# Three RMS norms of a long Trainium2 kernel: x is turned unscaled and split from PSUM, the scale is applied behind the matrices, and the gated unit's blocks change their order

## The chip, the cores and the metric

The kernel runs on one core of one Trainium2 chip. The metric is the device time of one execution in microseconds, smaller being better. The engines are named as in the profile: PE (TensorE) multiplies matrices, PEld is its load of the stationary operand, DVE is VectorE, ACT is ScalarE, POOL is GpSimd, SP is SyncE.

## What is computed

Three residual layers over 256 tokens of width 1024, in fp32: layer 0 mixes by attention, layer 1 by a state-space unit (S5) whose output goes through a gated unit, and each ends in a feed-forward of width 4096. A third layer with conditioning, convolution, window attention and an expert part of 16,384 rows follows. What the change touches, cut from the reference:

```
def rms_norm(x, g):
    y = xf * lax.rsqrt(jnp.mean(xf * xf, axis=-1, keepdims=True) + EPS)
    return (y * g).astype(x.dtype)

def s5_mixer(...):
    ...
    val, gate = jnp.split(g @ w_glu, 2, axis=-1)
    return val * jax.nn.sigmoid(gate)

def sq_relu_mlp(h, w1, w2):
    return jnp.square(jax.nn.relu(h @ w1)) @ w2

for layer in range(DEPTH):                      # DEPTH = 2
    h = rms_norm(x, mix_norm_g[layer])
    ...                                         # attn_mixer begins with h @ w_in; or s5_mixer
    x = x + sq_relu_mlp(rms_norm(x, ffn_norm_g[layer]), w_ff1[layer], w_ff2[layer])
```

The norm has a scale per token, r = 1/sqrt(mean square + EPS), and a gain per channel, g. A product with h is r times the product with x * g; squared and relu'd it is r squared times.

## The kernel before

Every engine has a program written out by hand (`tensor_program`, `vector_program`, `scalar_program`, `gpsimd_program`, `sync_program`); the order of the work is the order of that code, and semaphores (`Signal`, `Bank`) join the programs. x lies in `xr`, 128 tokens by 2 by 1024.

**Matrices at fp32 precision.** Both operands of a large product are cut into a high part in fp32r (`w_hi`, `HH`) and a low rest (`w_lo`, `HL`); `three` (L523) issues hi*hi, hi*lo and lo*hi. Weights stream through a ring of four units of 512 KB (SP, L515), two chunks of 512 columns each. `cut_ahead` on ACT makes the high part (L1823), `cut_ahead` on DVE the low one (L1069), up to three chunks ahead of the chunk that PE is at, into four places; ACT may overwrite a place when PE has used it (`w_used`). `lin_tok` keeps the turned activations stationary and has eight chunks per block of 512 columns; `lin_T` keeps the weights stationary, two chunks per half (m) of a pair j of output blocks. In `ff1` a chunk is twelve matmuls of 256 columns. `weave` and `side` put small steps of other work between the chunks: in `ffn(0)` the tables of S5 (`s5_tables`, on PE, ACT and DVE), in `ffn(1)` the conditioning vector (`ada_step`: ACT fetches `w_ada`, DVE sums it).

**A norm** (`norm` in three programs; numbers 0 before `w_in`, 1 before `ff1_0`, 2 before S5, 3 before `ff1_1`, 4 and 5 later) is a chain over three engines: ACT squares both token halves with a sum; DVE takes mean and EPS; ACT the root; DVE the reciprocal and four scalings of x into `hn`; PE turns `hn` in sixteen 128x128 transposes (L544) into banks 4 to 7; DVE multiplies each bank by the gain into SBUF; ACT cuts HH, DVE cuts HL; only then `lin_tok` or `lin_T` begins:

```
for n in range(4):                                           # DVE, L1103
    ts(hn[:, t, half], xr[:, t, half], ss[:, t:t + 1], None, ALU.mult).then_inc(*scaled("hn", s, n))
tt(dst, pb(4 + n, 4, 128), B(g.unsqueeze(2), [128, 4, 128]), ALU.mult)
copy(HH[sl], hT[sl]).then_inc(*ahi_cut("norm", s, n))        # ACT
low(HL[place(3)], hT[place(3)], HH[place(3)], "norm", s, 3)  # DVE
```

**Around the norms.** At the start ACT issues both halves of x and then `small` (the identity for the transposes and the gains); SP waits for both halves of x before the first weights; `norm(0)` on PE waits for `small`. Before norm 1 stands `mix_out("w_o", ...)`: two blocks of eight chunks, each followed by two additions to x on DVE. Before norm 3 stands `glu`: blocks in the order values 0, gates 0, values 1, gates 1; behind each gates block ACT takes two sigmoids and DVE, per token half, multiplies by the values in PSUM and adds to x. `ffn` ends with four additions from PSUM to x (`add_to_x`).

## Time and profile before

| | |
|---|---|
| median of 3 runs | 1603.62 us (1602.17 to 1605.49) |
| profiled execution, its own time | 1605.25 us |
| its span in the profile | 1602.7 us |
| PE, PEld, DVE, ACT, POOL busy | 1475.8, 1361.2, 1166.7, 798.5, 326.9 us |
| DMA | 346.61 MB, 216 GB/s in the mean |

The span runs from the first to the last instruction of the profiled execution. PE is busy for 92% of it, so what is left lies in short stretches in which PE waits; a view by stretches shows them, and the timeline shows what fills them.

### The profile page before, as it was taken

How to read it: one execution, taken by the hardware profiler on the slowest of the kernel's cores; microseconds unless marked ns; L12 is line 12 of the kernel's file. 1: busy time of each engine (PE TensorE's matmuls, PEld its weight loads, DVE VectorE, ACT ScalarE, POOL GpSimd, SP SyncE). 2: the span in 40 equal slices, each digit the busy share in tenths (PEclk: the TensorE clock that was granted, in tenths of full speed). 3: DMA queues.
4: the chain of work that ended last, by engine and by line, in shares of the span. 5: the costliest groups of instructions: out<-in, count | busy, mean ns of one | idle time of the engine just before them, and what ended most of it. 6: DMA issues, size and time to landing. Idle time of an engine off the chain costs nothing.

```text
span 1602.7 us, 28608 instructions
## 1 busy us (share of the span) xinstructions
PE 1475.8 (92%) x10976; PEld 1361.2 (85%) x10976; DVE 1166.7 (73%) x2281; ACT 798.5 (50%) x1623; POOL 326.9 (20%) x380
## 2 busy tenths in 40 slices
PE   6788999998788999979879999999999989999998
PEld 5566998676777997858769899999999989999997
DVE  5575986575747887976775599367777768888887
ACT  4585786553655444545645210243333346666664
POOL 6520001000000000000000000178878811111110
PEclk9999999999999999989899999999999999999999
DMA  6214454453046888844235466699999968988884
GB/s 216 82 40 140 132 171 136 129 156 122 30 156 203 294 290 282 308 172 165 79 106 162 144 205 200 236 330 364 368 356 326 349 224 300 308 305 299 311 309 146
DMA packets 102197, 346.61 MB, mean 216 GB/s; under 512 B 11360, under 2 KB 11488, under 8 KB 101808
## 3 DMA queue, kind: packets, MB, share of 16 engines
q1 hardware_dynamic: 67680, 245.00, 45.8%
q0 software_dynamic: 19264, 70.84, 12.4%
q10 hardware_dynamic: 15120, 28.95, 5.5%
q8 instruction: 89, 1.46, 0.4%
q14 instruction: 44, 0.36, 0.1%
HBM read 343.70 MB, written 1.05 MB: 215 GB/s over the span
## 4 chain that ended last, share of the span: by engine, by line
PE 69%; DVE 14%; DMA 6%; ACT 5%; POOL 4%; issue 3%; ACTq 0%; DVEq 0%
PE ps L521 67%; DVE arena L1069 6%; ACT arena L1820 2%; DVE w_lo L1069 2%; DMA arena<-in_v_rows,arena 2%; POOL arena L2598 2%; POOL arena L2587 2%; DVE arena L1075 2%; DMA arena<-in_u_rows,arena 2%; ACT w_hi L1823 1%; DVE arena L1072 1%; DMA arena<-in_peer_v 1%; DVE act_hi_lo L1069 1%; ACT arena L1823 1%; PE ps L759 0%
## 5 line engine op out<-in xcount | busy, mean ns | idle before, releaser
L1069 DVE TENSOR_TENSOR w_lo<-arena,w_hi 128x512 fp32r<-128x512 f32 x680 | 457.0, 687 | 236.1 <-ACT w_hi L1823 232.8
L1823 ACT ACTIVATE w_hi<-arena 128x512 fp32r<-128x512 f32 x680 | 418.6, 626 | 360.7 <-PE ps L521 264.3
L521 PE MATMUL ps<-act_hi_lo,w_hi 128*128 128x256 f32 (+1 forms) x2496 | 567.8, 318 | 13.8 <-DVE act_hi_lo L1069 12.5
L521 PE MATMUL ps<-arena 128*128 128x192 f32 (+12 forms) x4952 | 520.7, 286 | 36.8 <-DVE arena L1069 11.3
L521 PEld LDWEIGHTS ps<-arena 128*128 128x128 f32 (+3 forms) x4952 | 484.3, 166 | 68.4 <-issue 26.1
L521 PE MATMUL ps<-act_hi_lo,w_lo 128*128 128x192 f32 (+1 forms) x1760 | 466.6, 265 | 0.0
L521 PEld LDWEIGHTS ps<-act_hi_lo,w_hi 128*128 128x128 f32 x2496 | 424.4, 191 | 19.2 <-issue 15.8
L521 PE MATMUL ps<-w_hi,act_hi_lo 128*128 128x512 f32 (+2 forms) x960 | 318.1, 403 | 33.3 <-ACT w_hi L1823 10.3
L521 PEld LDWEIGHTS ps<-act_hi_lo,w_lo 128*128 128x128 f32 x1760 | 339.0, 193 | 0.0
L521 PEld LDWEIGHTS ps<-w_hi,act_hi_lo 128*128 128x128 f32 x960 | 186.1, 195 | 83.1 <-issue 25.2
L1069 DVE TENSOR_TENSOR arena<-arena 128x512 f32<-128x512 f32 (+13 forms) x315 | 197.1, 631 | 43.6 <-ACT arena L1820 28.3
L521 PE MATMUL ps<-w_lo,act_hi_lo 128*128 128x512 f32 (+2 forms) x480 | 190.6, 397 | 0.0
L1823 ACT ACTIVATE arena<-ps 128x512 f32<-128x512 f32 (+16 forms) x202 | 81.6, 430 | 181.8 <-DVE arena L1069 132.1
L1820 ACT ACTIVATE arena<-arena 128x128 f32<-128x128 f32 (+7 forms) x300 | 140.8, 480 | 60.6 <-DVE arena L1069 23.6
L1075 DVE SCALAR_TENSOR_TENSOR arena<-arena 128x512 f32<-128x512 f32 (+6 forms) x176 | 152.4, 866 | 15.2 <-DMA arena<-in_v_rows,arena 11.0
L1820 ACT ACTIVATE arena<-ps 32x128 f32<-32x128 f32 (+20 forms) x201 | 80.3, 421 | 149.3 <-PE ps L521 147.4
L2587 POOL DMA_INDIRECT arena<-in_u_rows,arena x64 | 83.1, 1299 | 249.4 <-DVE arena L1696 223.6
L2587 POOL DMA_INDIRECT arena<-in_v_rows,arena x64 | 81.7, 1276 | 239.1 <-DVE arena L1075 183.7
L2439 POOL TENSOR_TENSOR arena<-arena 128x32 f32<-128x32 f32 (+1 forms) x122 | 44.6, 379 | 373.9 <-ACT arena L1823 343.4
L1713 DVE SCALAR_TENSOR_TENSOR arena<-arena 128x1024 f32<-128x1024 f32 x64 | 78.3, 1233 | 42.4 <-DMA arena<-in_u_rows,arena 27.3
L521 PEld LDWEIGHTS ps<-w_lo,act_hi_lo 128*128 128x128 f32 x480 | 93.6, 195 | 17.4 <-issue 0.5
L1069 DVE TENSOR_TENSOR arena<-ps,arena 128x512 f32<-128x512 f32 (+18 forms) x154 | 82.4, 552 | 24.6 <-PE ps L521 17.6
(81 smaller groups left out, 632.8 us busy)
## 6 DMA issues: line engine op xcount, KB each, us to landing
arena<-in_w_ff SPq DMA_DIRECT2D x128, 512.0 KB, 4.0
arena<-in_peer_u SPq DMA_DIRECT2D x128, 512.0 KB, 5.2
arena<-in_peer_v SPq DMA_DIRECT2D x128, 512.0 KB, 5.6
arena<-in_w_ada ACTq DMA_DIRECT2D x96, 256.0 KB, 4.4
arena<-in_w_glu SPq DMA_DIRECT2D x16, 512.0 KB, 3.6
arena<-in_peer_wq SPq DMA_DIRECT2D x16, 512.0 KB, 3.6
arena<-in_w_in SPq DMA_DIRECT2D x12, 512.0 KB, 3.6
arena<-in_w_conv SPq DMA_DIRECT2D x12, 512.0 KB, 3.6
```

The lines of the kernel that those rows point to most:

```text
L521: return e.matmul(o, l, r, start=start, stop=stop)
L1069: return e.tensor_tensor(o, a, b, op)
L1072: return e.tensor_scalar(o, a, s1, s2, op0, op1) if op1 is not None else e.tensor_scalar(o, a, s1, None, op0)
L1075: return e.scalar_tensor_tensor(out=o, in0=a, scalar=s, in1=b, op0=op0, op1=op1)
L1713: ins = e.scalar_tensor_tensor(out=slot, in0=slot, scalar=1.0, in1=row_h[:, g], op0=ALU.mult, op1=ALU.mult, accum_out=a)
L1820: return e.activation(o, a, f, **k)
L1823: return e.activation(o, a, ACT.Copy)
L2439: return e.tensor_tensor(o, a, b, op)
L2587: e.indirect_dma_start(row_slot(n), None, T[f"{kind}_rows"], bass.IndirectOffsetOnAxis(ap=row_at[:, p:p + 1].bitcast(U32), axis=0)).then_i ...
L2598: ins = e.tensor_scalar(ob[:, k, :], iota, ibT[:, n:n + 1], gT[:, n:n + 1], ALU.is_equal, ALU.mult)
```

## The change

What it does, part by part:

- **Norms 0, 1 and 3.** PE turns x itself (`turn_x`), sixteen transposes of 128 channels by 128 tokens; ACT cuts HH straight from PSUM with the gain as its per-partition scale (`cut_x`, eight instructions of 256 columns); DVE makes HL in one instruction, PSUM times gain less HH (`low_x`, eight). `hn`, the four scalings and the four multiplications by the gain are gone from these norms.
- **Their scale** moves behind the products. Norm 0: squares, root and reciprocal stand inside the first `w_in` block, and each of the four `proj` evictions multiplies by r. Norms 1 and 3: squares on ACT behind pair j = 2 of `ff1`, mean and reciprocal on DVE behind j = 6 (r squared, so no root), and the four additions at the end of the feed-forward become `stt` with that scale.
- **First half of x early.** `turn_half` puts eight transposes of norm 1 inside the second `w_o` block, `glu` eight of norm 3 inside its last block. The other eight follow the block.
- **First pair of ff1** (`first_pair`) takes the chunks in the order 0, 2, 1, 3, so that the first two need only channel blocks 0 to 3.
- **Gated unit.** Order of blocks: values 0, gates 0, gates 1, values 1 (also of the weights in memory). The sigmoids of gates 1 lie before the last block.
- **Start.** `small` is issued by SP first; SP waits for one half of x for its first weight unit and for the other for the second. ACT cuts four pieces of x, one weight chunk, then the other four.

The diff, cut to its core (some new helpers appear twice in it and are shown once):

```
+    X_BANK = {0: (4, 5, 6, 7), 1: (4, 5, 6, 7), 3: (6, 7, 4, 5)}
...
     def sync_program(e):
+        e.dma_start(V(OFF_SM, SMN), T["small"]).then_inc(small_in, 16)
         e.wait_ge(x_in[0], 16)
-        e.wait_ge(x_in[1], 16)
         for i, (_, source, _, _) in enumerate(plan):
+            if i == 1:
+                e.wait_ge(x_in[1], 16)
...
+        def turn_x(s, half, ready):                               # PE
+            for t in range(2):
+                ready(t)
+                for k in range(4 * half, 4 * half + 4):
+                    if t == 0 and k % 2 == 0:
+                        bank[X_BANK[s][k // 2]].empty(e)
+                    ins = e.transpose(turned_x(s, k)[:, t, :], xr[:, t, 128 * k:128 * k + 128], ident)
+                    if t == 1 and k % 2 == 1:
+                        ins.then_inc(*turned("x", s, k // 2))
...
+            a = chunk(name)                                       # PE, first_pair
+            bank[0].take(e, *use)
+            piece(a, 0, 0).then_inc(*w_used())
+            b, c = chunk(name), chunk(name)
+            piece(c, 1, 0)
+            w_used()
+            piece(b, 0, 4).then_inc(w_used()[0], 2)
+            piece(chunk(name), 1, 4).then_inc(*w_used())
...
-                run(lin_tok("w_glu", 512, (0, 1) if j == 0 else (4, 5), ready, "glu_values", j))
-                run(lin_tok("w_glu", 512, (2, 3), ready, "glu_gates", j))
+            run(lin_tok("w_glu", 512, (0, 1), ready, "glu_values", 0))
+            run(lin_tok("w_glu", 512, (2, 3), ready, "glu_gates", 0))
+            run(lin_tok("w_glu", 512, (2, 3), ready, "glu_gates", 1))
+            for k, _ in enumerate(lin_tok("w_glu", 512, (4, 5), ready, "glu_values", 1)):
+                if k == 4:
+                    turn_x(3, 0, lambda t: e.wait_ge(*glu_v["added", 0, t]))
+            turn_x(3, 1, lambda t: e.wait_ge(*glu_v["added", 1, t]))
...
-        mix_out("w_o", mixed0, ((0, 1), (2, 3)))
+        mix_out("w_o", mixed0, ((0, 1), (2, 3)), turn_half())
+        turn_x(1, 1, lambda t: e.wait_ge(*bank[2 + t]["w_o", 1]))
...
+        def low_x(s, ks):                                         # DVE
+            for k in ks:
+                if k % 2 == 0:
+                    e.wait_ge(*ahi_cut["x", s, k // 2])
+                stt(HL[:, k, :]..., turned_x(s, k), x_gain(s)[:, k:k + 1], HH[:, k, :]..., ALU.mult, ALU.subtract)
...
-            norm(s, sm("ffng")[:, 8 * layer:8 * layer + 8], 0)
+            low_x(s, range(8))
...
+                if j == 6:
+                    mean_square(s)
+                    e.wait_ge(*stats["norm_var", s])
+                    inverse(s)
...
-                    add_to_x(2 + 2 * t + hf, t, hf, None)
+                    stt(xs, pb(bk, 512), stat(f"norm{s}", 3)[:, t:t + 1], xs, ALU.mult, ALU.add)
...
+        def cut_x(s, ks):                                         # ACT
+                ins = act(HH[:, k, :]..., turned_x(s, k), ACT.Copy, scale=x_gain(s)[:, k:k + 1])
...
-            free = turned["norm", s, 3]
+            free = glu_v["added", 1, 1]
...
-            norm(s, x_ready, 0)
+            cut_x(s, range(8))
...
+                if j == 2:
+                    squares(s, x_ready, [V(6144, 1024), V(7168, 1024)])
```

**PE, end of the second w_o block.** `ps<-arena` are the transposes, `act_hi_lo,w_hi` the first matmuls of `ff1_0`; `scaled` is DVE's scaling of `hn`, `bank2_empty` and `bank3_empty` its additions to x, `act_lo_cut` its low parts. Before:

```order
L521 MATMUL ps<-w_lo,act_hi_lo 128x512
L521 MATMUL ps<-w_hi,act_hi_lo 128x512
L544 MATMUL ps<-arena 128x128 [waits bank4_empty,scaled]
L544 MATMUL ps<-arena 128x128 x3
L544 MATMUL ps<-arena 128x128 [waits bank5_empty,scaled]
L544 MATMUL ps<-arena 128x128 x3
L544 MATMUL ps<-arena 128x128 [waits bank6_empty,scaled]
L544 MATMUL ps<-arena 128x128 x3
L544 MATMUL ps<-arena 128x128 [waits bank7_empty,scaled]
L544 MATMUL ps<-arena 128x128 x3
L521 MATMUL ps<-act_hi_lo,w_hi 128x256 [waits act_lo_cut,bank0_empty,weights_lo,weights_hi]
```

Now, inside the block:

```order
L551 MATMUL ps<-w_hi,act_hi_lo 128x512
L589 MATMUL ps<-arena 128x128 [waits bank4_empty,bank0_empty]
L589 MATMUL ps<-arena 128x128
L589 MATMUL ps<-arena 128x128 [waits bank5_empty]
L589 MATMUL ps<-arena 128x128
L589 MATMUL ps<-arena 128x128 [waits bank1_empty]
L589 MATMUL ps<-arena 128x128 x3
L551 MATMUL ps<-w_hi,act_hi_lo 128x512 [waits weights_lo,weights_hi]
```

and behind it:

```order
L551 MATMUL ps<-w_lo,act_hi_lo 128x512
L551 MATMUL ps<-w_hi,act_hi_lo 128x512
L589 MATMUL ps<-arena 128x128 [waits bank6_empty,bank2_empty]
L589 MATMUL ps<-arena 128x128
L589 MATMUL ps<-arena 128x128 [waits bank7_empty]
L589 MATMUL ps<-arena 128x128
L589 MATMUL ps<-arena 128x128 [waits bank3_empty]
L589 MATMUL ps<-arena 128x128 x3
L551 MATMUL ps<-act_hi_lo,w_hi 128x256 [waits bank0_empty,act_lo_cut,weights_lo,weights_hi]
L551 MATMUL ps<-act_hi_lo,w_hi 128x256
L551 MATMUL ps<-act_hi_lo,w_lo 128x256
L551 MATMUL ps<-act_hi_lo,w_hi 128x256 [waits act_lo_cut]
```

The sixteen transposes no longer wait for `scaled`; eight moved in front of the block's last three chunks, and the other eight wait only for the additions.

**ACT, start of the program.** `arena<-arena 128x1024` are the squares, `act_hi_lo` the high parts of x, `w_hi` the first weight chunks. Before:

```order
L2323 DMA arena<-in_x 128x1024 x2
L2324 DMA arena<-in_small 128x973
L1820 ACT_TABLE_LOAD
L1820 ACTIVATE arena<-arena 128x1024 [waits x_in0]
L1820 ACTIVATE arena<-arena 128x1024 [waits x_in1]
L1820 ACT_TABLE_LOAD
L1820 ACTIVATE arena<-arena 128x2 [waits stats]
L1823 ACTIVATE act_hi_lo<-arena 128x4x128 [waits bank4_empty]
L1823 ACTIVATE act_hi_lo<-arena 128x4x128 [waits bank5_empty]
L1823 ACTIVATE act_hi_lo<-arena 128x4x128 [waits bank6_empty]
L1823 ACTIVATE act_hi_lo<-arena 128x4x128 [waits bank7_empty]
L1823 ACTIVATE w_hi<-arena 128x512 [waits ring_in0]
```

Now:

```order
L2465 DMA arena<-in_x 128x1024 x2
L1944 ACT_TABLE_LOAD
L1944 ACTIVATE act_hi_lo<-ps,arena 128x256 [waits turned]
L1944 ACTIVATE act_hi_lo<-ps,arena 128x256
L1944 ACTIVATE act_hi_lo<-ps,arena 128x256 [waits turned]
L1944 ACTIVATE act_hi_lo<-ps,arena 128x256
L1947 ACTIVATE w_hi<-arena 128x512 [waits ring_in0]
L1944 ACTIVATE act_hi_lo<-ps,arena 128x256 [waits turned]
L1944 ACTIVATE act_hi_lo<-ps,arena 128x256
L1944 ACTIVATE act_hi_lo<-ps,arena 128x256 [waits turned]
L1944 ACTIVATE act_hi_lo<-ps,arena 128x256
L1947 ACTIVATE w_hi<-arena 128x512
```

The squares and the root with its table load left the front; the first weight chunk stands between the two halves of x.

## Rows read from the trace of the kernel before

**Rows 1.** The page, chain of work that ended last, shares of span by engine.
```profile
PE 69%; DVE 14%; DMA 6%; ACT 5%; POOL 4%; issue 3%; ACTq 0%; DVEq 0%
```

**Rows 2.** Windows: length, busy and count for PE, PEld, DVE, ACT, POOL, then PEclk, DMA share, GB/s.
```profile
0.00:16.40 16.40, 3.50 (x16) 3.28 (x16) 7.90 (x19) 9.12 (x15) 8.18 (x19) 0.98 0.82 302
...
157.40:166.20 8.80, 2.87 (x16) 2.50 (x17) 7.09 (x18) 5.07 (x10) 0.00 (x0) 0.79 0.16 53
...
180.00:220.00 40.00, 40.00 (x339) 40.00 (x338) 36.75 (x60) 32.95 (x56) 0.00 (x0) 1.00 0.58 171
...
490.00:500.80 10.80, 3.80 (x18) 3.33 (x17) 8.34 (x17) 6.74 (x12) 0.00 (x0) 0.68 0.13 47
...
1010.00:1280.00 270.00, 264.60 (x1828) 261.96 (x1827) 183.07 (x344) 94.00 (x270) 204.53 (x160) 0.99 0.93 338
```

**Rows 3.** Timeline, program's start: start us, us, engine, line, operation [idle before it <- releaser].
```profile
5.65 52.67 SPq L515 DMA_DIRECT2D arena<-in_w_in  x14
...
7.37 0.93 POOL L2442 DMA_DIRECT2D arena<-in_w_uq  x1 [6.94 <-DMA arena<-in_small]
...
16.48 0.76 PE L521 MATMUL ps<-w_hi,act_hi_lo 128*128 128x512 f32 x1 [3.86 <-ACT w_hi L1823]
```

**Rows 4.** DMA issues, first 7 us: count, KB each, median us to landing.
```profile
arena<-in_w_in SPq DMA_DIRECT2D x3, 512.0 KB, 4.5
```

**Rows 5.** Timeline, end of w_o and begin of ff1 of layer 0.
```profile
156.97 0.39 PE L521 MATMUL ps<-w_hi,act_hi_lo 128*128 128x512 f32 x1
...
159.04 0.17 DVE L1069 TENSOR_TENSOR arena<-arena 128x8 f32<-128x8 f32 x1
...
166.20 0.77 PE L521 MATMUL ps<-act_hi_lo,w_hi 128*128 128x256 f32 x2 [1.70 <-DVE act_hi_lo L1069]
```

**Rows 6.** Timeline, end of w_glu and begin of ff1 of layer 1.
```profile
490.14 1.09 ACT L1820 ACTIVATE arena<-ps 128x512 f32<-128x512 f32 x2 [0.67 <-PE ps L521]
...
492.82 0.69 DVE L1069 TENSOR_TENSOR arena<-arena 128x512 f32<-128x512 f32 x1
...
500.77 0.48 PE L521 MATMUL ps<-act_hi_lo,w_hi 128*128 128x256 f32 x2 [1.07 <-DVE act_hi_lo L1069]
```

**Rows 7.** Windows, PE alone: length, busy and count, PEclk, DMA share, GB/s.
```profile
19.00:22.10 3.10, 3.10 (x8) 0.50 0.78 267
...
166.20:169.30 3.10, 3.10 (x14) 0.50 0.00 0
...
490.00:496.00 6.00, 0.10 (x1) 0.80 0.23 85
```

**Rows 8.** Groups of ACT by shape: count | busy us, mean ns | idle before <- releaser.
```profile
L1823 ACT ACTIVATE w_hi<-arena 128x512 fp32r<-128x512 f32 x664 | 411.3, 629 | 357.5 <-PE ps L521 261.1 <-DVE arena L1075 48.4 <-DMA arena<-in_peer_v 36.3
...
L1820 ACT ACTIVATE arena<-ps 128x512 f32<-128x512 f32 x36 | 21.3, 598 | 17.1 <-PE ps L521 16.1
...
L1820 ACT ACTIVATE arena<-arena 128x1024 f32<-128x1024 f32 x12 | 12.6, 1051 | 9.7 <-DVE arena L1069 8.5 <-DMA arena<-in_x 0.9
L1820 ACT ACTIVATION_READ_ACCUMULATOR arena<-arena 128x1 f32 x64 | 12.2, 191 | 0.0
...
L1823 ACT ACTIVATE arena<-ps 128x256 f32<-128x256 f32 x15 | 5.5, 376 | 3.0 <-DVE arena L1069 3.0
...
L1820 ACT ACTIVATE arena<-ps,arena 64x256 f32<-64x256 f32 x2 | 0.9, 469 | 0.5 <-PE ps L619 0.5
```

**Rows 9.** Groups of DVE by shape, same columns.
```profile
L1069 DVE TENSOR_TENSOR w_lo<-arena,w_hi 128x512 fp32r<-128x512 f32 x664 | 448.9, 691 | 227.0 <-ACT w_hi L1823 223.9
...
L1075 DVE SCALAR_TENSOR_TENSOR arena<-arena 128x512 f32<-128x512 f32 x88 | 65.6, 745 | 3.1
L1069 DVE TENSOR_TENSOR arena<-ps,arena 128x512 f32<-128x512 f32 x68 | 44.7, 684 | 14.6 <-PE ps L521 12.2 <-ACT arena L1820 1.8 <-PE ps L544 0.3
...
L1075 DVE SCALAR_TENSOR_TENSOR arena<-arena,ps 128x256 f32<-128x256 f32 x8 | 3.5, 475 | 1.8 <-PE ps L521 1.8
```

**Rows 10.** Timeline: stationary loads of PE's six rank transposes.
```profile
37.83 0.64 PEld L587 LDWEIGHTS ps<-arena 128*128 128x128 f32 x6 [2.33 <-DVE arena L1072]
```

More of the change, by code:

```diff
@@ L1839, in cut_ahead, with squares, norm @@
                 at["cut"] += 1
-        def norm(s, ready, at_raw, shift=False, cut=True, early_root=True):
+        def cut_x(s, ks):
+            for k in ks:
+                if k % 2 == 0:
+                    e.wait_ge(*turned["x", s, k // 2])
+                ins = act(HH[:, k, :].rearrange("p (t n) -> p t n", t=2), turned_x(s, k), ACT.Copy,
+                          scale=x_gain(s)[:, k:k + 1])
+                if k % 2 == 1:
+                    ins.then_inc(*ahi_cut("x", s, k // 2))
+        def squares(s, ready, places):
+            for t in range(2):
+                ready(t)
+                ins = act(places[t], xr[:, t, :], ACT.Square, accum_out=stat(f"norm{s}", 3)[:, t:t + 1])
+            ins.then_inc(*squared("norm", s))
+        def norm(s, ready, at_raw, shift=False, cut=True):
             hT = V(at_raw, 8, 256)
@@ L2075, in s5_tables @@
             e.wait_ge(*got_ssm)
-            e.wait_ge(*turned["norm", 1, 3])
+            e.wait_ge(*squared["norm", 0])
             for ri in range(2):
@@ L2323, in scalar_program @@
             e.dma_start(xr[:, t, :], T["x"][128 * t:128 * t + 128, :]).then_inc(x_in[t], 16)
-        e.dma_start(V(OFF_SM, SMN), T["small"]).then_inc(small_in, 16)
-        norm(0, lambda t: e.wait_ge(x_in[t], 16), 22528, early_root=False)
-        run(in_block(0))
+        cut_x(0, range(4))
+        at["last"] = 0
+        cut_ahead()
+        at["last"] = end["peer_wq"] - 1
+        cut_x(0, range(4, 8))
+        for k, _ in enumerate(in_block(0)):
+            if k == 2:
+                squares(0, lambda t: e.wait_ge(x_in[t], 16), [hn[:, 0], hn[:, 1]])
+            elif k == 4:
+                ss = stat("norm0", 3)[:, 0:2]
+                e.wait_ge(*stats["norm_var", 0])
+                act(ss, ss, ACT.Sqrt).then_inc(*rooted("norm", 0))
         side = rank_norms()
```

115 lines of the change are left out of this document (93 added, 22 removed).

## The prediction

> **What bounds the kernel now.** I read the chain of work that ended last first [rows 1]: PE holds 69% of the span, so a gain must come out of stretches in which PE stands idle. The windows show where these are [rows 2]. From 180 to 220 us, inside `ff1_0`, PE is busy for 40.00 of 40 us; in 0 to 16.4 us it works 3.50 us, in 157.4 to 166.2 us 2.87 us, in 490.0 to 500.8 us 3.80 us. These are norms 0, 1 and 3, in which squares, mean, root, scalings, transposes, gain, high cut and low cut follow one another. The timelines give their ends: the first matmul of `w_in` starts at 16.48 [rows 3]; `w_o` sends its last matmul at 156.97 and `ff1_0` starts at 166.20 [rows 5]; behind `w_glu` the sigmoids start at 490.14 and `ff1_1` at 500.77 [rows 6]. All later work waits for PE, so what one of the three stretches loses should leave the span whole. The sum goes against the profiled execution's own time, 1605.25 us, which is 1.63 us above the median of the runs.
>
> **Prices.** A transpose costs 0.64/6 = 0.107 us at full clock [rows 10], and I take twice that at half clock. A matmul of 256 columns costs 40.00/339 = 0.118 us at full clock [rows 2] and 3.10/14 = 0.221 at half [rows 7]. An ACT piece of x (256 columns out of PSUM, with a scale read from SBUF) has its nearest row at 0.469 us [rows 8]; neighbours overlap a little, so I take 0.39 apiece in a row, with 0.376 (the eviction without such a scale) and 0.469 as the bounds. This is the place for a rule that speaks against the change: the Trainium skill, ScalarE: Activation LUTs, What ACT_TABLE_LOAD costs, says that each scale or bias read through a pointer adds a fixed time to an ACTIVATE. The two rows agree, 469 against 376 ns; by the rule eight scaled pieces cost more than four plain ones of 512 columns, and were they all on the path the sum would be smaller by eight times that difference at each norm, about 0.7 us. A DVE low piece has its row at 0.475 us [rows 9]; 0.41 apiece in a row, bounds 0.33 and 0.475.
>
> **Start (norm 0).** Before, x and `small` leave from one queue and `small` lands at 6.94 [rows 3]. Now SP sends `small`, but the three transfers share the same DMA engines, so I put it at 6.3 and no earlier. PE then turns x: sixteen transposes at half clock, the first pair of channel blocks ready at about 7.9. ACT cuts four pieces until 9.5. The first weight unit is issued when x's first half lands, about 5, and takes 4.5 us [rows 4]: 9.5 as well. Its high cut (0.63 [rows 8]) and low cut (0.69 [rows 9]) end at 10.9, and the first matmul starts at 11.0 instead of 16.48: **5.5 us** (bounds 4.0, should `small` or the unit land late, and 6.5). The second chunk's parts are ready at 13.3 to 14, when PE at half clock is through the first, 2.6 us for six matmuls. Squares (two of 1.05 us and a sum reading of 0.19 [rows 8]) and the root with its table load now stand between later chunks, where ACT is three chunks ahead. The clock: PE ran at 0.50 until 22.1 [rows 7], 5.6 us after its first matmul. Now 3.4 us of transposes stand closer before it; I take **0.7 us** for an earlier rise, bounds 0 and 2.5. POOL's chain of small operations starts with `small` and gains only 0.6 us, so DVE will wait some 1.5 us for its reciprocal near 39 us; PE has the rank matmuls there, and nothing on PE waits for it.
>
> **w_o to ff1_0 (norm 1).** Eight transposes move into the block: PE ends it 8 x 0.107 = 0.9 us later, and DVE's two additions and the three tiny operations of the conditioning behind them shift by as much: their end, 159.04 + 0.17 [rows 5], becomes 160.1. Four of the other transposes run behind each addition and are done by then. ACT has cut pieces 0 to 3 by then. One low piece, and `ff1_0` starts at 160.6 instead of 166.20: 5.6 us. Before, fourteen matmuls ran at half clock until 169.30 [rows 7], which cost 14 x (0.221 - 0.118) = 1.4 us. With 2.5 us of idle, broken by transposes, in place of 9 us, I expect full clock. Off goes 0.25, since the first four low pieces at 0.41 feed three matmuls each of 0.118. Together **6.7 us** (bounds 5.0 and 7.3). The order 0, 2, 1, 3 keeps PE from waiting for pieces 4 to 7: two chunks, 2.8 us, before the third is asked for.
>
> **Gated unit to ff1_1 (norm 3).** Again 0.9 us of transposes in the block. Before, the sigmoids started at 490.14 and the last addition, started at 492.82, ended at 493.5 [rows 6]. Now DVE starts at 491.0 without sigmoids before it, four operations of 0.68 us: 493.8. A low piece, and `ff1_1` starts at 494.4 instead of 500.77; with 0.25 off for the feed and nothing for the clock, which was back for 500.8: **6.1 us** (bounds 4.3 and 6.6). The conditioning's fetches move up with ACT's pieces and DVE's first sum waits for them, until about 499.3; the low parts that PE needs at 501.8 are then cut at 501.1, so this costs nothing, with 0.7 us to spare and a bound of 1.
>
> **What is added.** Squares behind pair 2: 2 x 1.24 us of squares, a relu of 0.60, a high cut of 0.63 and a low cut of 0.69 [rows 8, 9] make 4.4 us until the fourth chunk is ready, and PE has three chunks of 12 x 0.118, 4.3 us. I take 0.5 us in each feed-forward, **1.0 us** together (bounds 0 and 3, for in `ff1_0` DVE is busy 36.75 of 40 us [rows 2] and catches up slowly). The four additions with r squared cost 0.06 us more each (745 against 684 ns [rows 9]): **0.3 us** together, since DVE stands on the path there. Two table loads for the root leave the path and stand again ahead of norms 2 and 4, where ACT waits for PE: nothing, and 1.3 us each if that cover were gone.
>
> Sum: 5.5 + 0.7 + 6.7 + 6.1 - 1.0 - 0.3 = **17.7 us**. The profiled execution would be 1587.5, the median 1603.62 - 17.7 = **1585.9**. About 0.2% (3.2 us) is what a measurement of this kernel can tell from no change.
>
> **Rivals.**
> - *The clock stays low.* PE does little between 491 and 494.4, its eight transposes aside. In this stretch before, the granted clock fell from 1.00 to a mean of 0.80 within 490 to 496 [rows 7], so it fell inside this very gap. If it falls now just before `ff1_1`, and also behind the shorter gap at 158 to 160.6, and does not rise early at the start, this takes 1.5 to 2.9 + 1.5 + 0.7 us back, and with late landings at the start (1.5 us) the gain is 12 us: 1591.5. The Trainium skill, TensorE: Matmul & The Clock Gate, Part 1, has the activity watched in a free-running window, so that the moment is not tied to a gap's begin; by that rule the same gap may cost or spare the half clock, and the trace agrees: at half behind one norm, full behind another. Chance 0.17.
> - *More is won than I count*: clock up early at the start, no wait behind the squares, pieces at their lower bounds: 5.5 + 2.5 + 7.2 + 6.5 - 0.3 = 21.4 us, 1582.2. Chance 0.08.
> - *The change doesn't reach the end.* From 1010 to 1280 us DMA is busy 0.93 with 338 GB/s [rows 2]; if that stretch were set by transfers which start at a fixed time, gains ahead of it would shrink there. Against it: weights are fetched only when ring places come free, gathers when the selection is done, so both shift with PE. If half went: 8.9 us, 1594.7. Chance 0.03.
> - *Slower by a convoy in ff1.* If after the squares ACT and DVE cannot regain their lead, each chunk comes late, by the round from used place to new low part. It decides from 17.7 + 1.0 = 18.7 us over the 2 x 52 chunks left behind pair 2, that is 0.18 us of wait per chunk. At 0.25 it would be 26 us against 18.7: 1611 us. For it speaks DVE's 92% in `ff1_0`; against it PE's 40.00 of 40 beside that, and ACT's 32.95. Chance 0.02.
>
> The forecast has 0.70. For the range I take 1582.0 to 1591.5, which holds the forecast's bounded terms, the second rival and the better part of the first. Faster 0.97 (all cases but the convoy, less a little for errors of kind), within 0.2% 0.01, slower 0.02.
>
> **What the new profile would show.** First matmul of `w_in` near 11.0; of `ff1_0` near 154.4 (160.6 less the 6.2 us of the start), some 2.5 us behind the end of `w_o` instead of 9; of `ff1_1` some 3.5 us behind the end of `w_glu` instead of 10.6. Transposes of 0.9 us inside both blocks. No squares, root or scaling between. PE's waits behind pair 2 under 1 us. Wrong would be: a first matmul after 12.5, half clock for `ff1_0`, recurring waits of PE for `w_lo` in either `ff1`, or a later stretch that is longer than before.

## The result, and the profile after

| | before | changed | ratio (95% interval) |
|---|---|---|---|
| median | 1604.26 us (14 runs) | 1591.94 us (14 runs) | 0.9922 (0.9907 to 0.9938) |
| profiled execution, own time | 1605.25 us | 1589.46 us | |
| its span | 1602.7 us | 1587.6 us | |

The gain is 12.5 us (10.0 to 14.9) where 17.7 were forecast, and the median, 1591.94, lies 0.4 us beyond the forecast's range. The three stretches that [rows 2] showed as PE's gaps became short, much as forecast. The timeline of the changed kernel at the start:

```profile
5.62 18.69 SPq L545 DMA_DIRECT2D arena<-in_w_in  x9
5.70 0.93 POOL L2593 DMA_DIRECT2D arena<-in_w_uq  x1 [5.27 <-DMA arena<-in_small]
5.75 3.76 PE L589 MATMUL ps<-arena 128*128 128x128 f32 x16 [5.75 <-DMA arena<-in_x]
...
10.82 0.47 PE L551 MATMUL ps<-w_hi,act_hi_lo 128*128 128x512 f32 x1 [1.32 <-ACT w_hi L1947]
...
13.21 0.47 PE L551 MATMUL ps<-w_hi,act_hi_lo 128*128 128x512 f32 x1 [0.76 <-issue]
...
14.92 1.15 ACT L1947 ACTIVATE w_hi<-arena 128x512 fp32r<-128x512 f32 x2 [3.07 <-DMA arena<-in_w_in]
...
16.37 0.47 PE L551 MATMUL ps<-w_hi,act_hi_lo 128*128 128x512 f32 x1 [1.53 <-ACT w_hi L1947]
```

The first matmul of `w_in` starts at 10.82 instead of 16.48 [rows 3] (forecast 11.0), and at full clock (0.47 us for the first, not 0.76). But ACT then waits 3.07 us for the second weight unit, and PE 1.53 us for the third chunk. The sum of the forecast has no such wait; only its first rival counts late landings at the start. The ends of norms 1 and 3:

```profile
156.38 1.29 DVE L1157 TENSOR_TENSOR arena<-ps,arena 128x512 f32<-128x512 f32 x2
157.12 1.25 PE L589 MATMUL ps<-arena 128*128 128x128 f32 x8 [0.78 <-DVE arena L1157]
...
158.73 0.47 PE L551 MATMUL ps<-act_hi_lo,w_hi 128*128 128x256 f32 x2 [0.35 <-DVE act_hi_lo L1163]
...
484.32 0.69 DVE L1157 TENSOR_TENSOR arena<-ps,arena 128x512 f32<-128x512 f32 x1
...
485.79 0.44 PE L589 MATMUL ps<-arena 128*128 128x128 f32 x2 [1.58 <-DVE arena L1157]
...
487.89 0.78 PE L551 MATMUL ps<-act_hi_lo,w_hi 128*128 128x256 f32 x2
```

PE ends `w_o` at 156.34 (157.12 less the idle 0.78) and starts `ff1_0` 2.4 us later; before, 8.8 us passed between the same two points (156.97 + 0.39 to 166.20 [rows 5]). It ends `w_glu` at 484.21 and starts `ff1_1` 3.7 us later; before, the sigmoids behind the last block began 10.6 us ahead of `ff1_1` [rows 6]. What is new lies ahead of the second gates block. Changed kernel, then the kernel before at the same chunk of `w_glu`:

```profile
457.14 1.28 ACT L1944 ACT_TABLE_LOAD   x1
...
458.44 1.08 ACT L1944 ACTIVATE arena<-ps 128x512 f32<-128x512 f32 x2
...
459.67 0.69 PE L551 MATMUL ps<-w_hi,act_hi_lo 128*128 128x512 f32 x1 [1.91 <-ACT arena L1944]
```

```profile
472.14 0.47 PE L521 MATMUL ps<-w_hi,act_hi_lo 128*128 128x512 f32 x1 [0.72 <-ACT w_hi L1823]
```

PE waits for two sigmoids (`arena L1944`), because gates 1 goes into the banks of gates 0. And the granted clock fell to half (0.50) at places where it had not fallen before. Windows of the changed kernel, PE alone (length, busy and count, PEclk, DMA share, GB/s):

```profile
33.10:36.50 3.40, 3.40 (x10) 0.50 0.73 236
70.70:74.00 3.30, 3.29 (x11) 0.50 0.62 166
87.80:101.30 13.50, 10.11 (x38) 0.50 0.00 0
...
459.80:463.10 3.30, 3.30 (x8) 0.50 0.00 0
487.10:490.40 3.30, 3.28 (x16) 0.50 0.28 74
524.70:528.00 3.30, 3.30 (x17) 0.50 0.75 268
```

and the kernel before, where PE did the same work (38.4 and 75.6 us answer to 33.1 and 70.7):

```profile
15.80:22.50 6.70, 6.02 (x14) 0.50 0.53 170
38.40:41.80 3.40, 3.40 (x18) 1.00 0.70 247
75.60:79.00 3.40, 3.40 (x23) 1.00 0.59 205
90.90:94.20 3.30, 3.19 (x12) 0.50 0.00 0
94.30:97.60 3.30, 0.63 (x5) 1.00 0.00 0
97.70:101.00 3.30, 3.30 (x13) 0.50 0.00 0
```

One caution on PEclk. The profile's record of the clock begins late (at 12.34 us in the profile of before, 9.19 in that of the changed kernel, 20.43 in before_again's), and a window ahead of that prints 1.00 even where PE ran at half clock (shown under before_again). There the spacing of the matmuls tells it: in `w_in` they start 0.43 us apart at half clock and 0.23 us apart at full clock. By this the changed kernel ran its first `w_in` matmuls at full clock in all its three profiles.

**A ruler for leads.** DVE cuts the same 680 low weight parts in the same sequence of stages in all kernels here. The end of the n-th cut, read from DVE's timeline, marks the same point of the program; its time in the first profile of before less its time in another profile is that profile's *lead*. All are in us:

| profile | cut 1, first | 13, w_in1 | 49, end w_o | 101, ff1_0 | 195, w_glu | 219, ff1_1 | 261, ff1_1 | 421, last ahead of experts | span |
|---|---|---|---|---|---|---|---|---|---|
| changed | 5.66 | 5.51 | 1.93 | 8.00 | 9.58 | 12.05 | 10.35 | 9.74 | 15.0 |
| after_again | 5.01 | 4.75 | 1.23 | 7.32 | 8.92 | 11.40 | 9.69 | 9.10 | 12.6 |
| after_third | 5.14 | 4.99 | 1.24 | 7.31 | 8.74 | 14.19 | 12.49 | 9.49 | 9.0 |
| before_again | -0.02 | 1.00 | 0.35 | -0.44 | 1.60 | 1.59 | 1.59 | -1.04 | 2.1 |
| start_only | 5.53 | 5.60 | 1.77 | 1.81 | 1.52 | 1.51 | 1.51 | 1.77 | 2.3 |
| norm1_only | -0.33 | -0.14 | -0.09 | 6.00 | 5.55 | 5.54 | 5.54 | 6.80 | 10.4 |
| norm3_only | -0.06 | 1.32 | -1.75 | -0.98 | -0.78 | 1.69 | -0.29 | -0.64 | -3.0 |
| old_order | 5.05 | 4.95 | 4.85 | 10.93 | 11.77 | 16.93 | 15.23 | 15.37 | 19.7 |
| no_squares | 4.87 | 5.65 | 4.13 | 11.05 | 11.14 | 13.58 | 11.95 | 11.36 | 12.9 |
| glu_banks | 4.96 | 3.88 | 1.70 | 7.79 | 9.49 | 16.16 | 15.95 | 16.90 | 14.8 |
| pool_late | 5.75 | 6.78 | 1.54 | 7.63 | 7.92 | 13.37 | 11.67 | 9.14 | 12.8 |
| start_pool | 4.90 | 6.54 | 4.78 | 5.56 | 4.66 | 4.66 | 4.67 | 6.08 | 10.3 |
| both | 5.17 | 6.03 | 2.76 | 8.83 | 10.42 | 17.09 | 15.40 | 14.59 | 24.9 |
| both_again | 5.03 | 5.89 | 2.57 | 8.66 | 10.27 | 16.90 | 15.19 | 14.34 | 13.9 |
| both_ada | 5.32 | 6.49 | 4.63 | 10.72 | 10.29 | 16.97 | 18.11 | 22.14 | 28.2 |

A growing lead means that the stretch was shorter than in the first profile of before. Behind cut 421 no kernel differs from another in its program; what the last column adds is the executions' own scatter (below).

### The profile page after: what moved, and what is told of

It is laid out like the page before. It is cut to its first block, busy times and chain, and to the rows that moved or that the text cites. A ratio compares the mean times of both kernels' runs of the same rounds, so it can differ in the third digit from the quotient of the medians.

```text
span 1587.6 us, 28566 instructions
## 1 busy us (share of the span) xinstructions
PE 1478.5 (93%) x10976; PEld 1361.9 (86%) x10976; DVE 1155.4 (73%) x2269; ACT 798.6 (50%) x1631; POOL 305.2 (19%) x380
## 4 chain that ended last, share of the span: by engine, by line
PE 63%; DVE 16%; DMA 8%; ACT 5%; issue 4%; POOL 3%; ACTq 0%; DVEq 0%
PE ps L551 62%; DVE arena L1157 6%; DMA arena<-in_u_rows,arena 5%; DVE w_lo L1157 3%; ACT arena L1944 2%; DVE arena L1163 2%; POOL arena L2738 2%; DMA arena<-in_v_rows,arena 2%; ACT w_hi L1947 1%; POOL arena L2749 1%; DVE arena L1160 1%; DVE arena L1828 1%; ACT arena L1947 1%; DVE act_hi_lo L1157 1%; DMA arena<-in_peer_v 1%
## 5 line engine op out<-in xcount | busy, mean ns | idle before, releaser
L551 PE MATMUL ps<-arena 128*128 128x192 f32 (+12 forms) x4952 | 522.0, 287 | 33.2 <-DVE arena L1157 10.3
L1947 ACT ACTIVATE arena<-ps 128x512 f32<-128x512 f32 (+16 forms) x194 | 77.5, 424 | 183.2 <-DVE arena L1157 134.2
L1944 ACT ACTIVATE arena<-arena 128x128 f32<-128x128 f32 (+7 forms) x296 | 140.0, 484 | 57.1 <-DVE arena L1157 22.1
L1163 DVE SCALAR_TENSOR_TENSOR arena<-arena 128x512 f32<-128x512 f32 (+6 forms) x176 | 152.3, 865 | 17.9 <-DMA arena<-in_v_rows,arena 13.9
L1944 ACT ACTIVATE arena<-ps 32x128 f32<-32x128 f32 (+20 forms) x201 | 80.1, 420 | 145.5 <-PE ps L551 143.9
L2738 POOL DMA_INDIRECT arena<-in_u_rows,arena x64 | 76.2, 1190 | 258.1 <-DVE arena L1811 222.7
L1157 DVE TENSOR_TENSOR arena<-ps,arena 128x512 f32<-128x512 f32 (+19 forms) x134 | 69.6, 534 | 25.1 <-PE ps L551 18.0
```

Of the source, the lines that this page charges most:

```text
L551: return e.matmul(o, l, r, start=start, stop=stop)
L1157: return e.tensor_tensor(o, a, b, op)
L1163: return e.scalar_tensor_tensor(out=o, in0=a, scalar=s, in1=b, op0=op0, op1=op1)
L1944: return e.activation(o, a, f, **k)
L1947: return e.activation(o, a, ACT.Copy)
L2738: e.indirect_dma_start(row_slot(n), None, T[f"{kind}_rows"], bass.IndirectOffsetOnAxis(ap=row_at[:, p:p + 1].bitcast(U32), axis=0)).then_i ...
```

## The experiments

Each was timed beside the kernel before on one chip, and its ratio is against those runs. Medians are compared directly only where two kernels ran side by side: after_again, glu_banks, pool_late and both; before_again, start_only, norm1_only and norm3_only; after_third, both_again, old_order and no_squares; both_ada and start_pool.

**The changed kernel again (after_again).** No edit.

> The changed kernel itself, for a second profile and a second set of runs. Two theories of the 3.7 us that were lost between the first block of w_in (lead over the kernel before 5.66 us) and the end of w_o (lead 1.93 us). A, moved clock drops: PE does the same work there, and only the stretches at granted clock 0.50 fall at other places (33.1 to 36.5, 70.6 to 74.0, 87.7 to 101.4 us in the first profile); then this second profile has the same operations and waits but drops at other places, and the lead at the end of w_o differs by 1 to 4 us from 1.93. B, a fixed wait: some operation comes later than before by the change's own order; then the lead at the end of w_o is again 1.9 within 0.3 us. Both expect the 1.91 us of idle of PE ahead of the second gates block to be there again, within 0.1 us, and a time of 1592 within 3 us.

1590.72 us, 0.9912 (0.9895 to 0.9929). Half clock fell at the same places, 0.6 us later; lead at the end of w_o 1.23, outside the band of either theory (A asked for other places, B for 1.9 within 0.3), and the idle time of 1.91 us is there. What follows: the loss of 3.7 us behind the first block came again (5.01 - 1.23 = 3.8), but B's reason (an operation that comes late) doesn't hold either: PE's idle time between cuts 13 and 49 is 22.0 us in the changed kernel and 21.8 in the kernel before; only its work at half clock is more, 20.3 us (20.0 here) against 12.8.

**Other banks for the gated unit (glu_banks).**

```
-            run(lin_tok("w_glu", 512, (2, 3), ready, "glu_gates", 1))
-            for k, _ in enumerate(lin_tok("w_glu", 512, (4, 5), ready, "glu_values", 1)):
+            run(lin_tok("w_glu", 512, (4, 5), ready, "glu_gates", 1))
+            for k, _ in enumerate(lin_tok("w_glu", 512, (2, 3), ready, "glu_values", 1)):
```

(and the same banks in the sigmoids and in DVE's products)

> The second gates block goes into banks 4 and 5 and the second values block into banks 2 and 3, nothing else. Theory A, the new order of blocks made a wait: the second gates block had to wait until the sigmoids of the first had read banks 2 and 3 (1.91 us of idle of PE at 459.67, and half clock until 463.16 behind it). Then that idle falls to below 0.8 us, the value of the kernel before, and the lead over the kernel before at the first chunk of ff1_1 is 2 to 3 us more than in the changed kernel: 1589 to 1590 us against 1592. Theory B, the idle belongs to the weights (the high cut behind table load and sigmoids on ACT comes late): idle stays at 1.5 us or more and the time is the changed kernel's within 1 us.

PE's wait in its timeline, and the window behind it:

```profile
462.65 0.47 PE L551 MATMUL ps<-w_hi,act_hi_lo 128*128 128x512 f32 x1 [0.73 <-ACT w_hi L1947]
```

```profile
462.60:466.00 3.40, 3.35 (x15) 1.00 0.65 202
486.00:489.00 3.00, 3.00 (x27) 1.00 0.86 271
```

Theory A is shown for the wait: 0.73 us as before the change. From cut 195 to 219 the lead now grows by 6.67 us, where the changed kernel gets 2.47, 4.2 us more where 2 to 3 were expected; the clock stays up in both places. The whole time, 1590.15 us, 0.9907 (0.9885 to 0.9928), doesn't show it: its six runs spread from 1582 to 1592, and its profile loses 5 us in the last stretch, see below.

**Later fetches of the rank matrices (pool_late).**

```
-        e.dma_start(V(RANK, 2, 768), T["w_uq"].rearrange("k p n -> p k n")).then_inc(rank_in, 16)
-        e.dma_start(V(RANK + 1536, 1024), T["w_ukv"]).then_inc(rank_in, 16)
...
             expo(False)
+            e.dma_start(V(RANK, 2, 768), T["w_uq"].rearrange("k p n -> p k n")).then_inc(rank_in, 16)
+            e.dma_start(V(RANK + 1536, 1024), T["w_ukv"]).then_inc(rank_in, 16)
```

> POOL issues its two fetches of the rank matrices (1.25 MB) only behind its first exponential, near 16 us, instead of at 5.7 us. Theory A: these fetches, which start 1.7 us earlier than before since small lands earlier, share the DMA engines with the second weight unit, so that it lands at 14.9 us, 9 us after its issue, and PE waits 1.53 us for the third chunk. Then the third chunk starts near 14.8 instead of 16.37, and the lead over the kernel before at the end of the first w_in block grows from 5.6 to 7 us. Theory B: the second unit is late because the other units of the ring are issued in the same moment and share the engines; then it lands at 13 us or later and less than 0.5 us is won. In the whole time A gives 1.5 us less, B nothing.

```profile
10.99 1.68 ACT L1947 ACTIVATE w_hi<-arena 128x512 fp32r<-128x512 f32 x3
13.73 0.63 ACT L1947 ACTIVATE w_hi<-arena 128x512 fp32r<-128x512 f32 x1 [1.05 <-PE ps L551]
```

ACT no longer waits for a weight unit; its waits are now for PE. The second unit's issue, in the changed kernel and then here (KB, us from issue to landing):

```profile
arena<-in_w_in SPq DMA_DIRECT2D x1, 512.0 KB, 8.1
```

```profile
arena<-in_w_in SPq DMA_DIRECT2D x1, 512.0 KB, 4.6
```

It was issued at 6.83 and 6.74, so it landed at 14.9 in the changed kernel (8.1 us after its issue, not 9 as the expectation says) and at 11.3 here. The lead at cut 13 is 6.78, against 5.51, 4.75 and 4.99: theory A, by 1.3 to 2.0 us. Over all profiles with the new start the lead there is 3.88 to 5.65 in the seven with early fetches and 5.89 to 6.78 in the five with late ones. At the end of w_o it is 1.54 all the same: half clock took it (PE worked 22.5 us at half clock between cuts 13 and 49, at 31.3 to 34.6 and 68.8 to 75.6 us among others). 1590.66 us, 0.9915 (0.9896 to 0.9934).

**Both edits (both, both_again).**

> Both edits together, later fetches of the rank matrices and other banks for the gated unit. If both theories A hold: 3.5 to 4.5 us less than the changed kernel, 1587.5 to 1588.5 us; if the clock takes a share back at other places, 1589 to 1591 us; if neither holds, 1592.

> Later fetches of the rank matrices and other banks for the second gates and values blocks, a second time, since the first time's ten or so runs spread over 12 us. Local terms that its first profile showed against the changed kernel: first w_in block 1 us shorter, w_glu 2.9 us shorter. Theory A, local terms reach the end: 3 to 5 us below the changed kernel of this call, with intervals apart. Theory B, what is won is given back at clock drops elsewhere: within 1.5 us of it.

1586.6 us, 0.9897 (0.988 to 0.9915), and 1585.46 us, 0.9893 (0.9869 to 0.9916), beside 1590.72 and 1592.84 for the changed kernel on the same chips. That is 4.1 and 7.4 us less, in the first case with intervals that overlap widely and in the second with intervals that still touch (theory A of both_again asked for intervals apart). The leads at cut 421 are 14.6 and 14.3, against 9.1 to 9.7. Theory A, by the traces more surely than by the times.

**The kernel before again (before_again).** Written with the changed kernel's code, and on each engine the same instructions as before.

> The kernel before, written with the changed kernel's code but all three norms and the gated unit as before: the same instructions in the same order on every engine. Wanted: a second profile of before. If its granted clock falls at the same places as in the first profile (15.8 to 22.6, 90.8, 97.7, 131.8, 162.5, 493.6 us), then the 3.7 us that the changed kernel loses between the first w_in block and the end of w_o are its own, for its two profiles also agree (drops at 33, 71 and 88 to 102). If before falls to half clock near 38 and 75 us too this time, they were luck of the first profile. The stretch from the last weight chunk ahead of the expert part to the first behind it was 426.3 us in the first profile of before, against 419.6 and 423.4 in two profiles of the changed kernel: theory A, this stretch merely varies, then 420 to 427 now; theory B, before is slower there, then 425 to 428. Time 1604 within 3 us.

1603.01 us, 0.9978 (0.996 to 0.9997): so much can two equal programs seem apart, and a difference of 3 us in this study is near the limit. Its windows:

```profile
16.50:20.40 3.90, 3.90 (x9) 1.00 0.53 159
20.50:24.40 3.90, 3.90 (x19) 1.00 0.41 141
37.60:40.90 3.30, 3.30 (x9) 0.50 0.66 236
68.30:71.60 3.30, 3.23 (x9) 0.50 0.04 11
92.20:102.30 10.10, 6.58 (x25) 0.50 0.00 0
```

PE was busy in both of the first two windows but did 9 matmuls in one and 19 in the other: half clock until 20.4 us, where the first profile of before had it until 22.6 (the 1.00 of the first window stands ahead of the record's begin). Then half clock came at 37.6 and 68.3, as it did near 33 and 71 in the changed kernel. norm3_only, with the same program up to there as well, left half clock at 19.7 and has it again at 36.9 and 74.4. norm1_only, the fourth, has it at the places of the first profile. So the places vary between executions of one program, and the first profile of before was a lucky one behind 22 us.

**One part of the change at a time (start_only, norm1_only, norm3_only).** The other norms, their part of `ff1` and, without norm 3, the order of the gated unit are as before.

> Only the start of the change: norm 0 unscaled with the scale at the evictions, small issued by SP, waits of SP apart. Norms 1 and 3, ff1 and the gated unit as before. Theory A, clock drops that stand at other places take most of it back: lead over the kernel before 5 to 5.7 us at the first chunk, near 2 us at the end of w_o, and 1.5 to 2.5 us in the whole time (1601.5 to 1602.5). Theory B, the start's lead reaches the end: 5.5 us less, 1598.5.

> Only norm 1: its transposes in and behind w_o, high and low parts straight from PSUM, first pair of ff1_0 in the order 0, 2, 1, 3, squares behind pair 2, the scale at the additions of ff2_0. Forecast of its terms: 6.7 less 0.5 for the squares less 0.15 for the additions, 6.0 us: 1598. In the changed kernel's profile the lead grew here by 6.1 us (from 1.93 at the end of w_o to 8.00 in ff1_0). Rival: part of it is given back at other clock drops behind (S5, w_glu); then 3 to 5 us, 1599 to 1601.

> Only norm 3 with the new order of the gated unit's blocks. Forecast of its terms: 6.1 less 0.5 less 0.15, 5.5 us: 1598.5. Theory of the new wait: the second gates block waits 1.9 us for the sigmoids of the first and half clock follows, together 2.9 us, and another clock drop in ff1_1 takes 1.4 us; then 1.0 to 3 us are left, 1601 to 1603.

| | median | ratio (95% interval) | lead at cut 421 |
|---|---|---|---|
| start_only | 1595.75 us | 0.9941 (0.992 to 0.9961) | 1.77 |
| norm1_only | 1597.87 us | 0.9951 (0.9927 to 0.9975) | 6.80 |
| norm3_only | 1602.74 us | 0.9989 (0.9968 to 1.001) | -0.64 |

Norm 1 is as forecast. Norm 3 brings nothing as it stands: from cut 195 to 219 its lead grows by 2.47, the number of the changed kernel, and 1.98 go again until cut 261. start_only's profile shows what theory A expects, its times (6 to 13 us less) more than either theory: the profiled execution, 1602.2 us, was the second slowest of ten. The size of the start's part in the times stays uncertain by some 3 us.

**The old order of blocks, half of x still turned in the last block (old_order).**

```
-            run(lin_tok("w_glu", 512, (2, 3), ready, "glu_gates", 1))
-            for k, _ in enumerate(lin_tok("w_glu", 512, (4, 5), ready, "glu_values", 1)):
+            run(lin_tok("w_glu", 512, (4, 5), ready, "glu_values", 1))
+            for k, _ in enumerate(lin_tok("w_glu", 512, (2, 3), ready, "glu_gates", 1)):
```

> The changed kernel with the gated unit's blocks as before: values 0, gates 0, values 1, gates 1; half of x is turned inside the last block as in the change. Theory: the new order costs 1.9 us of wait and 1 us of half clock ahead of the second gates block, and saves on the other side the two sigmoids behind the last block, 1.1 us on the path. So the old order shall be shorter in w_glu by 2 to 3 us and longer between the last matmul of w_glu and ff1_1 by 1.1 us (or 1.1 plus 3.4 us of half clock in ff1_1): together 0.5 to 1.8 us below the changed kernel. Rival: the order is worth its price, then it is slower than the changed kernel by up to 1 us.

```profile
460.37 0.47 PE L551 MATMUL ps<-w_hi,act_hi_lo 128*128 128x512 f32 x1 [0.73 <-ACT w_hi L1945]
```

At the end of the last block PE waits 2.14 us for the additions instead of 1.58, since two sigmoids stand ahead of them again:

```profile
479.24 1.08 ACT L1942 ACTIVATE arena<-ps 128x512 f32<-128x512 f32 x2 [0.67 <-PE ps L551]
...
481.34 2.44 PE L589 MATMUL ps<-arena 128*128 128x128 f32 x8 [2.14 <-DVE arena L1157]
```

The lead grows by 5.16 from cut 195 to 219: more than the 2.47 of the new order, less than its 6.67 with other banks. So the new order is worth 1.5 us once its wait is gone, and costs 2.7 as it stands where half clock follows its wait. Whole: 1587.93 us, 0.991 (0.9886 to 0.9933). Its profile also ran `w_in` at half clock until 17.4 us, then had no half clock until 85.6 us, and kept 4.85 us at the end of w_o:

```profile
11.40:17.30 5.90, 5.87 (x14) 1.00 1.00 398
17.40:60.00 42.60, 36.94 (x147) 1.00 0.37 110
60.00:85.60 25.60, 17.09 (x99) 1.00 0.42 135
```

(The first window stands ahead of the clock's record; its 14 matmuls in 5.87 us are the half-clock spacing.) With `w_in` at half clock until then PE did not wait for the second unit, 0.1 us of idle time between cuts 1 and 13 against 2.4 in the changed kernel, and its lead at cut 13 is the same, 4.95. So while that unit is late, a full clock at the start only buys waiting.

**No squares (no_squares).** Squares, mean and EPS of norms 1 and 3 are left out.

> The squares, the mean and EPS of norms 1 and 3 are left out (the scale is taken from a constant); all else as in the changed kernel. Theory: PE's 0.61 us of idle behind pair 2 of ff1_0 goes, nothing goes in ff1_1 at that place, and the 1.09 us of idle ahead of the conditioning's small matmuls near 523 us, with the half clock that follows it, stays, because DVE is late there for another reason. Gain 0.6 us in the trace, nothing that the times can tell. Rival: the squares set DVE and ACT back for longer; then the idle near 523 falls to 0.74 us and the half clock behind it goes, together 2.3 us.

The 0.61 us of idle at 181.21 go, and the lead from cut 49 to 101 grows by 6.92 instead of 6.07: the squares cost 0.85 us in `ff1_0`. In `ff1_1` nothing changes; the idle time ahead of the conditioning's matmuls stays:

```profile
521.29 1.05 PE L551 MATMUL ps<-arena 128*128 128x1 f32 x8 [1.01 <-DVE arena L1163]
```

1590.92 us, 0.9922 (0.9896 to 0.9948): no difference in the times, as the theory had it.

**The changed kernel a third time (after_third).**

> The changed kernel a third time, beside the three others of this call. Its half clock fell at the same places in two profiles; the kernel before, whose four profiles had the same program until the end of w_o, did not agree with itself there (3.4 to 13.5 us of PE's work at half clock per stretch, places shifted, lead at the end of w_o 0, 0.35, -0.09 and -1.75 us). Expected: drops near 33 and 71 us again with 0.8 probability; lead at the end of w_o 1 to 3 us; time 1591 within 2 us.

1592.84 us, 0.9932 (0.9909 to 0.9955); lead at the end of w_o 1.24. Behind the 1.91 us of idle time the clock stayed up this time:

```profile
460.50:464.00 3.50, 3.49 (x15) 1.00 0.00 0
```

and the lead grew by 5.45 from cut 195 to 219 instead of 2.47. pool_late is the same (13.37 - 7.92). So the wait itself costs 1.2 us (6.67 - 5.45; before, PE idled 0.72 there too), and half clock behind it and at 487 the other 3.0, in four of six profiles with this wait. In the other two the new order, wait and all, stands 0.3 us ahead of the old one.

**The conditioning's sum used one step later (both_ada).** On top of both edits:

```
         def ada_step(m):                                  # PE
-
+            ada_use()
             for _ in range(2 - m):
-                ada_use()
                 ada_load()
```

(DVE takes PE's result two steps later)

> The version with other banks and later rank fetches, and in ff1_1 and ff2_1 the conditioning's sum is used by PE one step later than it is asked for now (by DVE two steps later), so that PE never asks for a sum that DVE has just begun. Theory A, the idle time brings the half clock: 1.09 us of idle near 518 us and the 3.4 us at half clock near 520.5 both go, the lead grows by 2.5 us in ff1_1, whole 1583 to 1585 us. Theory B, half clock falls there for another reason (it belongs to the stretch): idle goes, the half clock stays within 10 us of there, 1.1 us are won. Rival: DVE's wait for PE at the later place costs low parts, then PE idles there and nothing is won.

```profile
519.61 0.95 PE L551 MATMUL ps<-arena 128*128 128x1 f32 x8
```

```profile
500.00:560.00 60.00, 60.00 (x505) 60.00 (x504) 51.02 (x86) 30.82 (x54) 0.00 (x0) 1.00 0.91 304
```

against, in the version both,

```profile
500.00:560.00 60.00, 58.91 (x482) 58.71 (x481) 48.74 (x82) 29.29 (x52) 0.00 (x0) 0.97 0.86 284
```

Theory A: idle time and half clock both go here, and no idle row is left at the three like places up to 671 us (0.73 to 0.94 us of idle each in the version both; only the one at 621.66 had half clock with it). From cut 219 to 261 the lead grows by 1.1 us instead of falling by 1.7; from cut 219 to 421 it is 7.7 us more than in both and both_again, of which 3.7 us are the idle time itself. This is one profile, and between cuts 261 and 421 the two profiles of the kernel before differ by 2.6 us. 1578.9 us, 0.9819 (0.9793 to 0.9846), where 1583 to 1585 were expected: the best version. Its interval lies apart from that of the changed kernel (0.9907 to 0.9938) and from those of both and both_again; by the ratios it is some 16 us below the changed kernel, but the two did not run side by side.

Idle time alone does not bring half clock. A wait of the same length in glu_banks, and one as long at a later sum in the kernel before, had none behind it:

```profile
518.79 1.05 PE L551 MATMUL ps<-arena 128*128 128x1 f32 x8 [1.08 <-DVE arena L1163]
```

```profile
637.21 0.94 PE L521 MATMUL ps<-arena 128*128 128x1 f32 x7 [1.12 <-DVE arena L1075]
```

**The start with later fetches (start_pool).** pool_late's edit on start_only.

> Only the start of the change with the later fetches of the rank matrices; norms 1 and 3, ff1 and the gated unit as before. Leads over the kernel before at the first weight chunk: 5.0 to 5.7 us; at the third: 3.3 to 4.1 (start_only 1.48, since the second weight unit was late); at chunk 12: 5.9 to 6.8 (start_only 5.6); at the end of w_o 2.5 to 3 if half clock comes near 32 and 69 us as in the two profiles of the version with both edits, 4.5 to 5.5 if it stays away as it did in one profile of another version. Whole: 1 us below start_only if the late unit is a true loss, else the same.

Leads at cut 1 and 3 4.90 and 3.13, both a little under what was expected, at cut 13 6.54, at the end of w_o 4.78, with half clock near 68 us but none near 32. 1599.43 us, 0.9947 (0.9923 to 0.997): against start_only the times tell nothing, the trace shows the 0.9 us at cut 13.

## Why the prediction was off

**The step under all terms.** I wrote that all later work waits for PE, so that what one of the three stretches loses leaves the span whole. The stretches became shorter nearly as I said, but the work between them did not stay as it was: between cuts 13 and 49 the changed kernel gives back 3.6 us, and between 219 and 261 1.7. This is the last of my signs of being wrong, a later stretch that is longer than before. The first matmul after 12.5, half clock for `ff1_0` and recurring waits for `w_lo` did not come.

**Start, 5.5 us until the first matmul: right** (5.66, 5.01 and 5.14), by compensation in part. `small` landed at 5.4, not 6.3, and the first weight unit was issued at 5.62, not 5, and landed after 3.6 us, not 4.5. I had also misread a row: the 6.94 and 5.27 us at POOL's fetch are the length of its idle time; `small` landed at 7.07 before and at 5.41 now.

**Start, clock +0.7: the step that failed first.** I took only the first block's clock into account. The sum of both start terms, 6.2, is 4.5 us at cut 13 (5.05 in the mean of the seven profiles with this start and the early rank fetches, less 0.55, the mean of the four profiles with the old start) and 2.8 us at the end of w_o (2.41 less -0.37). In the changed kernel full clock in the first block was there at once, but ACT waited 3.07 us for the second unit, since POOL's fetches, which wait for `small`, moved up by 1.7 us and share the DMA engines with it. I had written that `small` gains little and looked only at POOL's arithmetic. pool_late shows this cause, and old_order shows that the clock is worth nothing there while the unit is late. Nor is the early clock the change's own for certain: start_only, no_squares and old_order, with the same start, ran at half clock until about 14 to 17.4 us, and glu_banks fell to half from 12.8 to 19.7. The rest went between cuts 13 and 49, where PE worked 18.7 us at half clock in the mean of those seven profiles and 15.4 in the mean of the four. The single values overlap (12.2 to 23.5 and 12.6 to 19.8), so whether the new start brings more half clock there or had bad luck stays open.

**w_o to ff1_0, 6.7 less 0.5 for the squares: right.** The lead grows by 6.07 to 6.09 in all three profiles of the changed kernel; the step's own signs (full clock, start 2.4 us behind the end of w_o) hold. The squares cost 0.85, not 0.5, and without them the step gives 6.9 where 6.7 was forecast.

**Gated unit to ff1_1, 6.1: the step that failed second.** The chain behind the last block is what I said, 3.7 us where 3.5 were forecast. But I counted the new order only where it helps. In the order values 0, gates 0, values 1, gates 1 the values block covered the sigmoids of gates 0; taken away, gates 1 must wait for banks 2 and 3. The diff shows the same banks twice in a row, and the forecast had to ask who empties them. It cost 1.2 us as wait and 3.0 as half clock in four of six profiles. With other banks the stretch gives 6.67, so the 6.1 without the wait was sound.

**What is added, 1.0: mis-sized, and in `ff1_1` for another reason.** The convoy did not come. The squares cost 0.85 us in `ff1_0` and next to nothing in `ff1_1` (1.70 less 1.63 in no_squares). But PE waits 1.09 us instead of 0.74 for the conditioning's sum near 523 us and half clock follows, together 1.6 to 2.0 us in nine of the ten profiles that have the new norm 3 with the conditioning as it was. The tenth is glu_banks, -0.2, with the same wait and no half clock. both_ada, which takes the wait away, has no half clock there either; so the wait goes with the half clock but does not bring it each time. Why DVE is 0.35 us later there stays open; the squares are not the reason. That the additions with r squared cost 0.3 us was not tried by itself.

**The sum.** 17.7 - 3.4 (start) - 3.8 (cut 195 to 261: forecast 5.6, mean of the changed kernel's three profiles 1.8) - 0.1 (norm 1 with its squares: 6.2 forecast, 6.1 measured) = 10.4. The three profiles lead by 9.4 at cut 421, the two of the kernel before by 0 and -1.04 (mean -0.5), which makes 9.9; the times say 10.0 to 14.9. The rival of the low clock gave 1591.5, the time that came. Half clock at the start of `ff1_1` (487.1 to 490.5, in two of the three profiles) and a late landing at the start were in it and came; half clock behind norm 1 and a late rise at the start didn't, and the gated unit's wait and the half clock between cuts 13 and 49 stood in no rival. That its number was met is luck in part. That the change's lead goes on to the end, against the third rival, holds: the means don't fall behind cut 421.

The Trainium skill, TensorE: Matmul & The Clock Gate, Part 1, calls the penalty run-variable since the activity is watched in a free-running window. The runs agree: four profiles with one and the same program until the end of w_o left half clock at 19.7 to 22.6 us, had it again near 38 or not, and differ by 2.1 us there.

## What to carry to other kernels

When an order of blocks changes, list for each block which banks or buffers it takes and whose read frees them: the block that was moved away may have been the cover of that read. When a transfer is made to land earlier, look at what waits for it, for these transfers then compete with the next one that PE needs. A short wait of PE can cost more than its length through the clock: taking away the one of 1.09 us gained 2.8 us, and the one of 1.91 us cost 4.2 us in four of six profiles; but many waits as short cost only themselves. Removing four of them (3.7 us of idle time in all) gained 7.7 us in one profile, more than the whole change at norm 1 (6.1).

When a profile says 1.00 for the clock at the start of a program, count the matmuls in the window before believing it.

## What the runs showed of the hardware

*The same program scatters by its own in the expert part.* both and both_again are one program. From cut 421 to 433 both took 416.7 us and both_again 426.5. Their timelines at the first chunk behind it:

```profile
1273.96 0.41 PE L551 MATMUL ps<-act_hi_lo,w_hi 128*128 128x384 f32 x1 [3.60 <-DVE act_hi_lo L1157]
```

```profile
1283.15 0.66 PE L551 MATMUL ps<-act_hi_lo,w_hi 128*128 128x384 f32 x1 [6.30 <-DVE act_hi_lo L1157]
```

with half clock behind the second. With DMA busy 0.97 from 1060 to 1160 us in both, I take landings for the source of it; this wasn't tried.

*Matmuls can be 2% slower at the same granted clock.* From 1320 to 1520 us, PE busy throughout (windows of glu_banks, then of both):

```profile
1320.00:1520.00 200.00, 200.00 (x1381) 1.00 0.87 298
```

```profile
1320.00:1520.00 200.00, 200.00 (x1409) 1.00 0.89 307
```

Behind cut 433 glu_banks, norm3_only and no_squares took 286.5 us each, the others 281.0 to 283.4: this made the 5 us that glu_banks lost in its last stretch. No row tells its cause.
